# Seven products in place of eight for seven more pairs of weight chunks (up projection, gating values) in a two-block float32 kernel

## What is computed

```python
# block 1: u, v are 4096 wide, zg too
proj = xn @ w_in
uv = jax.nn.gelu(proj[..., :2 * GMLP_WIDTH])
zg = proj[..., 2 * GMLP_WIDTH:]
u, v = jnp.split(uv, 2, axis=-1)
v = rms_norm(v, v_g)
...
# block 2, feed-forward, D_FF = 8192
hn = rmsnorm(x, norm_ffn_pre[l])
u = jnp.square(jax.nn.relu(jnp.einsum('bsd,df->bsf', hn, w_up[l])))
y = jnp.einsum('bsf,fd->bsd', u, w_down[l])
```

## Time and profile before

| | |
|---|---|
| median of 3 runs | 2559.22 us (2558.97 to 2559.31) |
| the profiled execution | 2559.44 us, of which its span is 2557.7 us |
| TensorE busy | 2551.5 us of the span, 11425 matmuls |
| VectorE busy | 1764.6 us (69%) |
| ScalarE busy | 1296.9 us (51%) |
| DMA to SBUF and back | 527.42 MB, 206 GB/s on average |

### The profile page before, as it was taken

One profiled execution on the slowest core, in us unless ns is written; L12 is line 12 of the kernel. 1 busy time (PEld: TensorE's weight loads), 2 busy tenths in 40 slices (PEclk: granted clock), 3 DMA queues, 4 the chain that ended last, 5 costly groups with the idle time before them and its releaser, 6 DMA issues.

```text
span 2557.7 us, 29454 instructions
## 1 busy us (share of the span) xinstructions
PE 2551.5 (100%) x11425; PEld 2115.1 (83%) x11425; DVE 1764.6 (69%) x2062; ACT 1296.9 (51%) x1554; POOL 34.8 (1%) x56
## 2 busy tenths in 40 slices
PE   9999999999999999999999999999999999999999
PEld 7888888888888888888888888888888888888887
DVE  5646565566666666776876777678678768778686
ACT  6554443444555555455454544445465455455463
POOL 1000000000000000000000000000020000000000
PEclk9999999999999999999999999999999999999999
DMA  8767766676776777778566787666757677666674
GB/s 271 216 189 210 205 202 196 190 208 204 215 220 196 215 196 200 219 227 230 165 181 181 206 223 201 203 206 198 244 174 223 195 216 212 215 196 224 204 231 141
DMA packets 534795, 527.42 MB, mean 206 GB/s; under 512 B 294896, under 2 KB 297824, under 8 KB 534656
## 3 DMA queue, kind: packets, MB, share of 16 engines
q1 hardware_dynamic: 531856, 518.09, 68.3%
q0 software_dynamic: 2384, 6.93, 1.1%
q10 hardware_dynamic: 416, 0.52, 0.1%
HBM read 488.24 MB, written 2.10 MB: 192 GB/s over the span
## 4 chain that ended last, share of the span: by engine, by line
PE 100%; ACT 0%; DVE 0%; issue 0%; ACTq 0%
PE bank L2312 30%; PE bank L2313 30%; PE bank L2314 30%; PE bank L2379 2%; PE bank L2380 2%; PE bank L2381 2%; PE bank L2498 1%; PE bank L2487 1%; PE bank L2477 1%; PE bank L2411 0%; PE bank L2420 0%; PE bank L2433 0%; PE bank L2426 0%; PE bank L2558 0%; PE bank L2545 0%; PE bank L2578 0%
## 5 line engine op out<-in xcount | busy, mean ns | idle before, releaser
L1255 DVE TENSOR_TENSOR t_wl<-t_stage,t_wh 128x1024 fp32r<-128x1024 f32 x844 | 1021.4, 1220 | 600.2 <-ACT t_wh L714 594.8
L714 ACT ACTIVATE t_wh<-t_stage 128x1024 fp32r<-128x1024 f32 x845 | 885.1, 1057 | 801.4 <-PE bank L2314 758.3
L2312 PE MATMUL bank<-t_wl,t_xth 128*128 128x512 f32 x2400 | 941.0, 392 | 0.5 <-DVE t_xtl L1297 0.5
L2314 PE MATMUL bank<-t_wh,t_xtl 128*128 128x512 f32 x2400 | 934.1, 389 | 0.0
L2313 PE MATMUL bank<-t_wh,t_xth 128*128 128x512 f32 x2400 | 934.0, 389 | 0.0
L2314 PEld LDWEIGHTS bank<-t_wh,t_xtl 128*128 128x128 f32 x2400 | 450.5, 188 | 94.1
L2312 PEld LDWEIGHTS bank<-t_wl,t_xth 128*128 128x128 f32 x2400 | 450.6, 188 | 93.9 <-DVE t_xtl L1297 0.9
L2313 PEld LDWEIGHTS bank<-t_wh,t_xth 128*128 128x128 f32 x2400 | 450.7, 188 | 92.5 <-issue 0.2
L2312 PE MATMUL bank<-t_wl,t_yth 128*128 128x512 f32 x914 | 355.6, 389 | 0.0
L2313 PE MATMUL bank<-t_wh,t_yth 128*128 128x512 f32 x914 | 355.1, 389 | 0.0
L2314 PE MATMUL bank<-t_wh,t_ytl 128*128 128x512 f32 x914 | 355.1, 389 | 0.0
(11 more groups left out here) (410 smaller groups left out, 1509.4 us busy)
## 6 DMA issues: line engine op xcount, KB each, us to landing
t_stage<-in_a_w_in_dram SPq DMA_DIRECT2D x192, 512.0 KB, 4.3
t_stage<-in_w_in_dram SPq DMA_DIRECT2D x168, 512.0 KB, 4.3
t_stage<-in_b_w_in_dram SPq DMA_DIRECT2D x128, 512.0 KB, 4.5
t_stage<-in_w_up_dram SPq DMA_DIRECT2D x92, 512.0 KB, 4.4
t_stage<-in_w_down_dram SPq DMA_DIRECT2D x90, 512.0 KB, 5.1
t_stage<-in_a_w_out_dram SPq DMA_DIRECT2D x64, 512.0 KB, 4.3
t_ubuf<-in_w_down_dram SPq DMA_DIRECT2D x38, 512.0 KB, 5.3
t_ubuf<-in_w_up_dram SPq DMA_DIRECT2D x36, 512.0 KB, 4.5
```

The lines of the kernel that those rows point to most:

```text
L714: e.activation(wh[:, j % N_SPLIT], stage[s], ACT.Copy).then_inc(*hi(j))
L1255: e.tensor_tensor(low, src, high.bitcast(F32), ALU.subtract).then_inc(*lo(j))
L2312: e.matmul(o, h, w_l, start=start, stop=False)
L2314: return e.matmul(o, l, w_h, start=False, stop=stop)
```

## The change

Seven more pairs: v (2, 3), (4, 5) and (6, 7), and up (q, 2) with (q, 3) for all four q. Of the up projection only chunks (0, 0) and (0, 1) stay plain. With them come the reading out of the new pairs (`v_sum`, `apart`, `together`), another order of relu, turning and splitting in the feed-forward, two more buffers for weights during v, and the token sums for the v and x3 pairs at an earlier place. Small parameters are transposed at group place 23 instead of 27, and the mask of the spatial weights is applied at another place in v.

```diff
@@ halved_pairs
-    return ([(("gm", c), ("ga", c)) for c in (2, 3)] +
+    return ([(("v", c), ("v", c + 1)) for c in (2, 4, 6)] +
+            [(("gm", c), ("ga", c)) for c in (2, 3)] +
             [(("w_out", 0), ("w_out", 1))] +
-            [((kind, q, c), (kind, q, c + 1)) for q in range(4) for kind, c in (("up", 0), ("down", 0), ("down", 2))
+            [((kind, q, c), (kind, q, c + 1)) for q in range(4) for kind in ("up", "down") for c in (0, 2)
              if (kind, q, c) not in (("up", 0, 0), ("down", 3, 2))])
@@ _program
+    if ("v", 2) in first_of:
+        opens["v", 1] = [(7, N_STAGE, None), (8, N_STAGE, None)]
+        closes["v", 6] = (7, 8)
@@ scalar: the gating values
-        def v_evac(c):
-            e.wait_ge(*used.at(end("v", c) - 1))
...
+        def v_gelu(c):
+            if ("v", c) not in pair_of:
+                e.wait_ge(*used.at(end("v", c) - 1))
...
+                if ("v", c) in pair_of:
+                    e.wait_ge(*vec.at("sum", "v", c, i))
+                e.activation(v_tile(c, i), v_tile(c, i) if ("v", c) in pair_of else accs("v", c)[i],
+                             ACT.Gelu_apprx_tanh, scale=sA[:, i:i + 1]).then_inc(*act("v", c, i))
@@ scalar: the up projection
+        def squared(q, c):
+
+            t = buf[c % 2]
+            slot(end("up", q, c))
+            if ("up", q, c) in pair_of:
+                e.wait_ge(*vec.at("sum", "up", q, c))
+            else:
+                e.wait_ge(*used.at(end("up", q, c) - 1))
+            for i in range(2):
+                e.activation(t[:, i, :], t[:, i, :] if ("up", q, c) in pair_of else accs("up", q, c)[i],
+                             ACT.Relu, scale=sF[:, i:i + 1]).then_inc(*act("up", q, c, i))
+            e.wait_ge(*act.at("up", q, c, 1))
+            e.activation(t, t, ACT.Square).then_inc(*act("squared", q, c))
...
+            squared(q, 1)
+            apart(first_of["up", q, 2], turned.at("up", q, 0))
+            if q:
+                up_high(q, 0)
+            up_high(q, 1)
+            squared(q, 2)
+            squared(q, 3)
+            apart(first_of["down", q, 0], vec.at("late", first_of["down", q - 1, 2], 1) if q >= 2 else None)
@@ vector: the gating values
+        slot(10)
+        split_sums(xth, xtl, mo[:, 0, 0:1024], mo[:, 0, 1024:2048], "v")
+        slot(11)
+        sum_low("v")
...
+        def v_sum(c):
+            slot(end("v", c))
+            e.wait_ge(*used.at(end("v", c) - 1))
+            for i in range(2):
+                e.tensor_tensor(v_tile(c, i), accs("v", c)[i], quarters(pair_of["v", c])[2 * (c % 2) + i],
+                                ALU.add).then_inc(*vec("sum", "v", c, i))
@@ vector: the up projection
+            slot(end("up", q, 1) + 2)
+            together(first_of["up", q, 2], turned.at("up", q, 1))
+            if q:
                 up_low(q, 0)
-            else:
-                up_turn(q, 0)
-                up_low(q, 0)
-                slot(end("up", 0, 1))
-                split_sums(xth, xtl, rowb.rearrange("p a b -> p (a b)"), vreg[:, 7168:8192], "x3")
...
+            up_low(q, 1)
+            for c in (2, 3):
+                up_sum(q, c)
+                up_turn(q, c)
             if q:
                 late(first_of["down", q, 0])
@@ freed (what TensorE waits for before it reuses the banks of a chunk)
+        if kind == "v" and name in pair_of:
+            return vec.at("sum", *name, 1)
@@ tensor
-        products(when(27))
+        products(when(23))
         t = bank_of(5)
```

More of the change, by code:

```diff
@@ L290, in low_after @@
     def low_after(q, c):
-        if ("up", q, c) in pair_of:
-            return 8 if c == 0 else 10
-        return 8 if c == 3 else 4
+        behind = 4 if q == 0 and c < 2 else (6, 10, 4, 8)[c]
+        return behind + end("up", q, c if q == 0 and c < 2 else c | 1) - end("up", q, c)
     def when(n):
@@ L695, in gpsimd @@
         for c in range(4):
-            e.wait_ge(*(vec.at("dr", c - 2, 1) if c >= 2 else used.at(where[first_of["up", 3, 0], P3])))
+            e.wait_ge(*(vec.at("dr", c - 2, 1) if c >= 2 else used.at(where[first_of["up", 3, 2], P3])))
             load_row(c, A["norm_ffn_post_2"][:, cols(c)], "ffn", c)
@@ L800, in scalar @@
             e.wait_ge(*x_in[c + 1].at(c + 1))
+            if c == 1:
+                sum_high("v")
             for i in range(2):
                 squares(hres[:, i, cols(c)], ssq[:, i, c:c + 1], "x", c, i)
+        apart(first_of["v", 2])
         slot(when(14))
-        v_evac(0)
-        for c in range(1, 8):
+        v_gelu(0)
+        slot(end("v", 1))
+        v_gelu(1)
+        for c in range(2):
+            slot(end("v", 1) + 3 + 2 * c)
+            v_squares(c)
+        for c in (3, 5, 7):
             slot(end("v", c))
-            if c == 2:
+            if c < 7:
+                apart(first_of["v", c + 1], vec.at("sum", "v", c - 1, 0))
+            slot(end("v", c) + 2)
+            if c == 3:
                 e.wait_ge(*vec.at("angles"))
@@ L1435, in angles @@
                                        op0=ALU.mult, op1=ALU.add).then_inc(*vec())
+        def v_sum(c):
+            slot(end("v", c))
+            e.wait_ge(*used.at(end("v", c) - 1))
+            for i in range(2):
+                e.tensor_tensor(v_tile(c, i), accs("v", c)[i], quarters(pair_of["v", c])[2 * (c % 2) + i],
+                                ALU.add).then_inc(*vec("sum", "v", c, i))
+        slot(end("v", 1))
+        together(first_of["v", 2])
         slot(when(20))
@@ L1458, in vector @@
         e.tensor_tensor(gmix, gc[:, 32:48], gc[:, 48:64], ALU.mult).then_inc(*vec("gmix"))
-        for p, n in ((0, 31), (1, 34)):
+        v_sum(2)
+        v_sum(3)
+        slot(end("v", 3) + 2)
+        together(first_of["v", 4], vec.at("sum", "v", 3, 1))
+        for p, n in ((0, 35), (1, 38)):
             slot(when(n))
@@ L1474, in vector @@
                 e.tensor_tensor(w, w, tri.unsqueeze(1).to_broadcast([128, 4, 128]), ALU.mult).then_inc(*vec("ws", q))
-        slot(when(64))
+        slot(when(41))
+        e.wait_ge(*pool.at("tri"))
+        ws_mask(0)
+        for c in (4, 6):
+            v_sum(c)
+            v_sum(c + 1)
+            if c == 4:
+                slot(end("v", 5) + 2)
+                together(first_of["v", 6], vec.at("sum", "v", 5, 1))
+                slot(end("v", 5) + 6)
+                ws_mask(1)
+        slot(end("v", 7) + 7)
         e.wait_ge(*square.at("v", 7, 1))
```

77 lines of the change are left out of this document (26 added, 51 removed).

## The result

The changed kernel takes 2621.15 us (median of 4 runs, 2620.19 to 2622.02), the kernel before on the same chip 2559.26 (2558.97 to 2559.42): ratio 1.024, 95% interval 1.022 to 1.026. It is **62 us slower**, where 2609 was forecast, in a range of 2592 to 2622. The profiled execution has a span of 2620.3 us against 2557.7.

What follows compares the result with a forecast made beforehand. TensorE was taken as the bound: number of matmuls times their distance. -9.5 + 16.8 + 25.2 + 5.8 + 6.7 + 5 = +50.0 on a span of 2557.7 gave 2609 us, range 2592 to 2622.

Steps and rivals of the forecast that it cites:

- Nearly all for L1276: Expected profile: TensorE's waits, up to some 60 us in all, are nearly all for VectorE's low at line L1276.
- first place: Up pair (q, 2) behind (q, 0), q = 1 to 3: waits 2.8 by plain group G, 0.4, 2.4; 5.6 each, +16.8.
- second place: Down pair (q, 0) behind the up pair, q = 1 to 3: waits 2.8 to G, 5.6 at P4; 8.4 each, +25.2.
- down, q = 0: Quarter 0's down pair, where `together` stands in place of `late`: 2.8 + 3.0, +5.8 us.
- up pair (0, 2): Quarter 0's up pair behind plain chunks: TensorE waits 1.2, 3.5, 1.0 and 0.9 for lows and token sums; +6.7 us.
- gating pairs: v pairs: (4, 5) and (6, 7) cost 0; (2, 3) late at the start, between 1 and 7, taken as +5 us.
- matmuls saved: Seven pairs, each with 186 matmuls for 192, 1.36 us saved per pair: -9.5 us.
- clock stays: Likeliest case, chance 0.50: stalls as walked, TensorE's clock not falling in the new gaps; 2609 us.
- the rival given 0.23: Clock falls in gaps before P4 of the down pairs, up to 4.1 us more each, three times; chance 0.23.
- up to 2621: Time, in us, at the upper end of the case that the clock falls, 12 us for three gaps added.
- Each place costs about half: Rival, chance 0.14: ScalarE's and VectorE's chains overlap better, first place 2.2, second 5.0; +20, 2579 us.

Runs made afterwards that it cites:

- e4: The changed kernel with unread filler matmuls in front of TensorE's long waits, fewer than in a first try (12, 4 and 8 per place, 6 in quarter 0): 2611.96 us.
- e10: e8 without the up projection's pair (0, 2), quarter 0's up projection ordered as in the kernel before: 2553.14 us, ratio 0.9975 to the kernel before.
- e2: The changed kernel with unread filler matmuls in front of TensorE's long waits (19, 7 and 12 per place, 9 in quarter 0): 2620.53 us.
- e5: The changed kernel with a paired up chunk's relu and square two groups later, VectorE's turn one, transfer two and adds one group later: 2574.56 us.
- e8: e5 with pair adds later, (0, 2)'s token sums before the norm's scale, parameter copies two groups sooner, first gating pair's adds two groups later: 2559.33 us.
- e11: The changed kernel with only ScalarE's relu and square of a paired up chunk two highs later, VectorE's turn, transfer and adds unmoved: 2591.15 us.

## Why the prediction was right, and where it was not

The mechanism and its places were right: waits for VectorE's lows at G, at P4 and behind P4, none for DMA. "Nearly all for L1276" was too much: of the 47.1 us in the four lines, 32.5 are for that low, 11.0 for the sums and 3.6 for the low of the token sums. e4 has the stalls without the clock, so its steps in the table, with the 1.36 us that a pair saves put back, can be set against the terms of the sum.

| term | predicted | measured in e4 | in the changed kernel |
|---|---|---|---|
| first place, each q | 5.6 | 5.7, 5.7, 5.7 | 7.3, 5.7, 7.3 |
| second place, each q | 8.4 | 9.2, 9.2, 9.5 | 11.1, 10.7, 11.1 |
| down, q = 0 | 5.8 | 5.9 | 7.5 |
| up pair (0, 2) | 6.7 | 7.7 | 8.4 |
| gating pairs | 5 | 3.0 | 2.9 |
| matmuls saved | -9.5 | -9.5 | -9.5 |

(q = 1 of the first place in e4: 16.4 - 12.1 + 1.4 = 5.7.) The sum was +50.0. The terms of e4 add up to +52.1, and 1.0 lies between the gating and the feed-forward stage, where nothing was changed, 0.8 of it at the wait in `w_out` that e10's rows show: +53.0, as the table has it.

**The step that failed** is the condition of the likeliest case, "clock stays". It fell, and the rival given 0.23 was the true one: the forecast of 2609 missed by 12 us, and e4 puts 9.2 of them on the clock. The range holds 2621.15 by less than 1 us. The rival itself was sized wrongly in both factors. It had three gaps, those at P4 of the down pairs, and 4.1 us each. There are eight stretches, in or behind gaps down to about 2 us, and each costs 1.2 in the mean (9.2 / 8). That its "up to 2621" is the time that was measured is luck: its 12 us for three gaps happen to equal the 9.2 of the clock and 3.0 of stalls and waits that the sum of +50.0 did not have. A stretch of 3.4 us holds 8 matmuls, 0.20 us further apart each, and loses 1.6 us, not 4.1, and part of the loss is taken off the next wait, since VectorE goes on meanwhile: the wait for the second sum of down's pair in q = 3 is 1.5 us in the changed kernel, behind a slow stretch, and 2.2 in e4, behind none. By the Trainium skill, "TensorE: Matmul & The Clock Gate", section "HAM oscillation", idle gaps put the clock back; the trace agrees, with 0.50 in the windows above and 1.00 in e4's where the gaps are filled.

One reading of the prediction was wrong beside this. The six rows of 256 columns in the earlier trace rows are three matmuls: one with two fp32 operands shows as two rows. So one takes 0.44 us at 1.00 (twelve took 5.34 in e4) and not 0.24. The factor of two between the start and the end stands, but e2's fillers were sized by the 0.24.

**The two places.** The idle time at P4 is 5.56, 5.08 and 5.59 us where 5.6 was worked out, and 2.07, 2.07 and 2.06 where 2.4 stood behind P4. The split was a little otherwise: the second sum's delay shows as 1.53 at (q, 3)'s first group and 0.78 at G, which I had as one 2.8. That `late` stands there in one block was right too, but half of what it cost was VectorE coming to it late: in e5, with the same block, the wait is 2.8 us.

**Up pair (0, 2).** 1.2 and 3.5 were predicted for its first two waits, 1.46 and 3.63 came. Its two small terms, 1.0 and 0.9, stand in e4 as 0.7 and 0.6 us of idle; in the changed kernel, where the clock is at 0.50 behind the 3.63, TensorE does not wait at these groups.

**Gating pairs.** +5 was too much. The trace has P5 of (2, 3) late by 0.6 us and not by 5: between 34 and 50 us no high of ScalarE waits for a load, where one had waited 2.40 us, and the bound to take lay nearer the lower one. That it was the two more buffers which brought the loads early was not tested by itself. One wait was priced at nothing, wrongly: the small parameters. TensorE writes them into bank 5 four groups sooner, but VectorE copies them out where it did, and P5 of the second pair waits 1.15 us for the bank (the copies end at 92.33 us, P5 starts at 92.43). e8 removed it, together with another of 0.6, and won 2.0.

**"Each place costs about half".** Its mechanism, chains of ScalarE and VectorE overlapping, was not in the kernel, but could be put there. What I took for given in the walk (strict order, 3.44 idle behind each sum) was the larger part of the cause: the kernel before could just afford it, the new pairs used up its slack, and e5 removes it without any new room on an engine.

Left open: how the 17 us between e11 and e5 divide over turn, transfer and adds, and whether some order would fit pair (0, 2). Neither was tried further.
